# Down products of the gathered experts: three fp32r passes of split operands in place of plain fp32

## The reference

```
expert_id = g_sel[:, None] * EXPERTS_PER_GROUP + top_i
combine = sum(one_hot(expert_id, N_EXPERTS) * w2[..., None], axis=1)
out = zeros_like(h)
for n in range(N_EXPERTS):
    a, b = split(h @ w_up[n], 2, axis=-1)          # 1024 -> 2 x 256
    out = out + combine[:, n:n + 1] * ((silu(a) * b) @ w_down[n])   # 256 -> 1024
```

## Time and profile before

| | |
|---|---|
| median of 3 runs | 2070.4 us (2069.82 to 2071.71) |
| the profiled execution | 2056.48 us, span 2054.7 us |
| mean granted TensorE clock of its span | 0.962 |
| TensorE busy (matmul) | 1899.3 us, 92% of the span |
| VectorE busy | 1187.3 us, 58% |
| ScalarE busy | 787.5 us, 38% |
| DMA | 391.10 MB, mean 190 GB/s |

### The profile page before, as it was taken

The page is one execution under the profiler, slowest core; times in us unless marked ns, Lnnn a source line. Parts: engine busy times, 40 slices in busy tenths (PEclk is TensorE's granted clock), DMA queues, the critical chain, the costliest instruction groups (busy, mean ns, idle before and its releaser), DMA issues.

```text
span 2054.7 us, 30793 instructions
## 1 busy us (share of the span) xinstructions
PE 1899.3 (92%) x12768; PEld 1710.6 (83%) x12768; DVE 1187.3 (58%) x1810; ACT 787.5 (38%) x1090; POOL 201.2 (10%) x95
## 2 busy tenths in 40 slices
PE   7697889799999998999899989998999989989998
PEld 6496868678876665999888869998999987869998
DVE  1399143366665655877527548776786337546442
ACT  3334441244444444433343324333443334324332
POOL 6327700000000000000130000000000140000000
PEclk9898999799999999999999989999999999989999
DMA  8144331256699987677541046777576541032441
GB/s 268 62 144 123 124 103 41 90 195 243 246 370 382 358 312 302 248 287 286 183 144 42 22 164 228 285 289 278 197 301 267 165 137 48 22 119 110 184 185 61
DMA packets 124458, 391.10 MB, mean 190 GB/s; under 512 B 11810, under 2 KB 72532, under 8 KB 95008
## 3 DMA queue, kind: packets, MB, share of 16 engines
q1 hardware_dynamic: 122048, 387.19, 50.7%
q0 software_dynamic: 1968, 0.90, 0.2%
q10 hardware_dynamic: 304, 1.06, 0.1%
HBM read 388.06 MB, written 1.05 MB: 189 GB/s over the span
## 4 chain that ended last, share of the span: by engine, by line
PE 81%; DVE 11%; ACT 3%; issue 2%; POOL 1%; DMA 1%; DVEq 0%; SPq 0%; ACTq 0%
PE bank L544 80%; DVE region L2136 2%; PE bank L578 1%; DVE hT L1814 1%; POOL slab_low L2595 1%; DMA slab<-in_w_up 1%; DVE region L1849 1%; DVE region L2101 1%; DVE slab_low L1836 0%; DVE xT L1947 0%; ACT w_hi L1413 0%; DVE region L2112 0%; ACT L1296 0%; DVE region L2115 0%; ACT region L1318 0%
## 5 line engine op out<-in xcount | busy, mean ns | idle before, releaser
L1836 DVE TENSOR_TENSOR slab_low<-slab,w_hi 128x2048 fp32r<-128x2048 f32 x152 | 348.0, 2291 | 188.6 <-ACT w_hi L1413 188.3
L544 PE MATMUL bank<-h_hi,w_hi 128*128 128x256 f32 x1408 | 403.6, 287 | 16.3 <-DVE h_lo L1829 16.3
L544 PE MATMUL bank<-h_lo,w_hi 128*128 128x256 f32 x1408 | 401.2, 285 | 0.0
L544 PE MATMUL bank<-h_hi,slab_low 128*128 128x256 f32 x1408 | 400.3, 284 | 0.0
L1413 ACT ACTIVATE w_hi<-slab 128x2048 fp32r<-128x2048 f32 x152 | 290.4, 1912 | 156.4 <-DMA slab<-in_w_up 81.0
L544 PEld LDWEIGHTS bank<-h_hi,w_hi 128*128 128x128 f32 x1408 | 270.6, 192 | 17.8 <-issue 17.8
L544 PEld LDWEIGHTS bank<-h_hi,slab_low 128*128 128x128 f32 x1408 | 270.3, 192 | 0.0
L544 PEld LDWEIGHTS bank<-h_lo,w_hi 128*128 128x128 f32 x1408 | 269.8, 192 | 0.0
L544 PE MATMUL bank<-gT_hi,d_hi 128*128 128x256 f32 x832 | 234.2, 281 | 0.0
L544 PE MATMUL bank<-gT_hi,d_low 128*128 128x256 f32 x832 | 233.8, 281 | 0.0
L544 PE MATMUL bank<-gT_lo,d_hi 128*128 128x256 f32 x832 | 233.7, 281 | 0.0
(11 more groups left out here) (309 smaller groups left out, 3278.2 us busy)
## 6 DMA issues: line engine op xcount, KB each, us to landing
slab<-in_w_ffn_in SPq DMA_DIRECT2D x88, 1024.0 KB, 8.1
slab<-in_w_up SPq DMA_DIRECT2D x64, 1024.0 KB, 9.0
region<-in_w_ada SPq DMA_DIRECT2D x112, 512.0 KB, 6.7
region<-in_w_ffn_out SPq DMA_DIRECT2D x44, 1024.0 KB, 5.0
region<-in_w_down SPq DMA_DIRECT2D x32, 1024.0 KB, 5.5
slab<-in_w_in SPq DMA_DIRECT2D x23, 1024.0 KB, 5.4
slab<-in_w_mix_in SPq DMA_DIRECT2D x20, 1024.0 KB, 9.7
hT<-in_w_ada SPq DMA_DIRECT2D x32, 512.0 KB, 5.9
```

Of the source, the lines that this page charges most:

```text
L544: return nc.tensor.matmul(o, lhsT, rhs, start=start, stop=True, skip_group_check=True)
L1836: V_.tensor_tensor(slab_low[slot][:, :], slab[slot][:, :], w_hi[h % 3][:, :].bitcast(F), ALU.subtract)\
```

## The change

The down products of the gathered units are made like those of the full ones, in three fp32r passes. Their matmuls keep the activations as the stationary operand and 512 weight columns as the moving one. `gT_few` goes; `gT_hi`, `gT_lo`, `d_hi` and `d_low` are used for all units. ScalarE and VectorE split the down weights of every unit, and do it ahead of the first half of the next up weights; the last unit's are split in the closing slot, ahead of the turned activations. `down_few` and `bank_free` wait for the low parts.

```diff
@@ down_few
-                pe.wait_ge(S[f"d_in{b}"], 16 * (unit.u // 2 + 1))
-                pe.wait_ge(S["gt_hi"], unit.steps[-1] + 1)
+                pe.wait_ge(S["dlo_ready"], split_units(unit.u))
+                pe.wait_ge(S["gt_lo"], low_steps(unit.steps[-1]))
...
-                rows_ = d_raw[b].rearrange("p (j d) -> p j d", j=2)
+                hi = d_hi[d_hi_of(unit)][:, :].rearrange("p (j d) -> p j d", j=2)
+                lo = d_low[b][:, :].rearrange("p (j d) -> p j d", j=2)
                 for j in range(2):
                     for half in range(2):
-                        m = mm(bank[2 + half][:, :], gT_few[b][:, j, :], rows_[:, j, half * 512:(half + 1) * 512],
-                               unit.x == 0 and j == 0)
+                        o, c = bank[2 + half][:, :], slice(half * 512, (half + 1) * 512)
+                        mm(o, gT_hi[b][:, j, 0:P], hi[:, j, c], unit.x == 0 and j == 0)
+                        mm(o, gT_hi[b][:, j, 0:P], lo[:, j, c])
+                        m = mm(o, gT_lo[b][:, j, 0:P], hi[:, j, c])
@@ bank_free
-                elif unit.split:
+                else:
                     pe.wait_ge(S["gt_lo"], low_steps(old))
-                else:
-                    pe.wait_ge(S["gt_hi"], old + 1)
@@ ScalarE, slots of segment 0
+                    if unit is not None and t == 0 and unit is not members[0]:
+                        down_high(UNITS[unit.u - 1])
                     if unit is not None and t == 0:
                         up_high(unit.halves[0] + 2)
-                        if unit is not members[0] and UNITS[unit.u - 1].split:
-                            down_high(UNITS[unit.u - 1])
+                    if unit is None:
+                        down_high(members[-1])
                     for x in pending:
                         turned_high(x)
@@ VectorE, slots of segment 0
+                    if unit is not None and t == 0 and unit is not members[0]:
+                        down_low(UNITS[unit.u - 1])
                     if unit is not None and t == 0:
                         up_low(unit.halves[0] + 2)
-                        if unit is not members[0] and UNITS[unit.u - 1].split:
-                            down_low(UNITS[unit.u - 1])
+                    if unit is None:
+                        down_low(members[-1])
                     for x in pending:
                         turned_low(x)
```

More of the change, by code:

```diff
@@ L170, in split, with gathered @@
     @property
-    def split(self):
-        return self.kind != "few"
+    def gathered(self):
+        return self.kind == "few"
 def plan():
@@ L368, in build @@
         gT_lo = [parts_at(f"gT_lo{b}", [2, T], silu_at + 4096 * b + 2048) for b in range(2)]
-        gT_few = [nc.alloc_sbuf_tensor_at(f"gT_few{b}", [P, 2, P], F, offset=silu_at + 4096 * b)
-                  for b in range(2)]
         act_s, gu_s = lnt[:, 0:T], lnt[:, T:2 * T]
@@ L498, in low_steps @@
         def low_steps(s):
-            return sum(len([x for x in u.steps if x <= s]) for u in UNITS if u.split)
+            return s + 1
         def split_units(u):
-            return sum(1 for x in UNITS[:u + 1] if x.split)
+            return u + 1
         def unit_of(s):
@@ L846, in down @@
             def down(unit, middle=None):
-                if unit.split:
+                if not unit.gathered:
                     down_split(unit, unit.steps[0] == SLOTS_OF[unit.seg][0][2], middle)
@@ L1457, in turned_high @@
                     src = place(s)[:, 0:T].rearrange("p (a b) -> p a b", a=2)
-                    dst = gT_hi[b][:, :, t * P:(t + 1) * P] if unit.split else gT_few[b][:, :, :]
+                    dst = gT_hi[b][:, :, t * P:(t + 1) * P]
                     nc.scalar.activation(dst, src, ACT.Copy).then_inc(S["gt_hi"], 1)
@@ L1968, in turned_low @@
                     unit = unit_of(s)
-                    if not unit.split:
-                        return
                     b, t = unit.u % 2, s - unit.steps[0]
```

## The result

The changed kernel takes 2098.4 us (median of 4 runs, 2097.25 to 2099.61), the kernel before on the same chip 2070.1 (4 runs): ratio 1.0138, 95% interval 1.012 to 1.0155, so 28.3 us (1.4%) slower. Forecast were 2088.8 us, +18.4, with a range up to 2098.0: direction and mechanism came true, the size did not; the time lies 0.4 us above the range.

What follows compares the result with a forecast made beforehand. TensorE, with DMA just behind it, was taken to bound the kernel; its savings would all turn into waits. Dense 7.3, gathered 7.9 and tail 3.2 sum to +18.4 us, giving 2088.8 us, range 2080 to 2098.

Steps and rivals of the forecast that it cites:

- What bounds before: Gathered units: TensorE (mean 9.43 us a unit) and DMA (9.3 us) set the pace together until the adaLN pieces end.
- The down product: Each gathered unit: 12 matmuls at 0.2325 us, 2.79 us for 3.42, saving 0.63 per unit, 15.1 us in 24 units.
- Dense part: Units 0 to 7: TensorE waits for turned_low, stalls of 1.35 and 0.45 us, plus 1.4 before down(8): +7.3 us.
- Gathered part: From down(8) to down(30): a closed loop through d_hi makes 22 periods take 224.1 us against 216.2: +7.9 us.
- the period of 9.85 us: Gathered units: d_hi starts 2.99 us after the down product, the next down product 6.86 later; 18 such periods.
- The end: Last down product, down(31), waits for d_hi, d_low and gT_lo; scatter 12.95 us after down(30) instead of 9.76: +3.2 us.
- a lower granted clock comes with the new idle time: TensorE, listed among the signs that the forecast is wrong; no size given.
- rival C: Gathered part: slabs come late inside the loop, 0.5 us more in 16 periods, 2097 us; chance 0.13.
- A: TensorE still sets the pace, with new VectorE and ScalarE work under its own: faster, 2055.3 us; chance 0.06.
- B: Gathered part: DMA sets the pace and covers the loop, 2069 to 2074 us, no measurable change; chance 0.07.
- D: Only the gathered loop or only the dense stalls come true: 2081 us; chance 0.12.

Runs made afterwards that it cites:

- fastest version: The changed kernel with turned_low and the copy of y ahead of up_low, two d_hi tiles and the closing slot reordered: 2058.8 us, ratio 0.9955 to the kernel before.
- version without the waits: The changed kernel with turned_low and the copy of y ahead of up_low and a second d_hi tile for odd gathered units: 2062.1 us, ratio 0.9975.
- b_again: The kernel before, unchanged, profiled a second time: 2065.1 us, ratio 0.9981, stage 373.2 us.

## Why the prediction was right, and where it was wrong

**What bounds before.** Right as to TensorE. Half wrong as to DMA. The 0.90 at 355 GB/s was a mean over unlike stretches of before, as the first 66 us and the last 69 us of the gathered part show:

```profile
576.00:642.00 66.00, 66.00 (x255) 44.99 (x254) 43.98 (x37) 30.79 (x28) 0.00 (x0) 1.00 0.98 386
723.00:792.00 69.00, 69.00 (x264) 47.50 (x263) 37.07 (x26) 31.90 (x30) 0.00 (x0) 1.00 0.83 322
```

In the first DMA was already busy for 0.98, at 386 GB/s. In the fastest version it gives 410 over the first 73 us, 4% more than the 394 of the forecast, so a unit there takes DMA 9.0 us, and not 9.3. Whether ScalarE's waits for slabs come from this or from loads that were asked for late, no run separates.

**The down product: right.** 12 matmuls at a pitch of 0.2325 us. TensorE's busy time between down(8) and down(30) fell by 8.6 us where 22 x 0.63 = 13.9 follows from the forecast, because matmuls at half clock and the ends of bursts, which no next matmul covers, count as busy too; in the version without the waits it is 200.8 for 214.1, 13.3 less.

**Dense part: +8.6 for +7.3.** The stalls are where they were forecast, and the run with the order alone shows them alone. Each is a little larger. From one down product to the next, a unit without an adaLN sum is 1.40 to 1.47 us longer than in before where 1.35 was forecast, and one with a sum 0.66 to 0.68 where 0.45 was. The idle times shown, 1.18 and 0.42, are shorter than these shifts because they begin only at the end of the last matmul, which takes 0.39 us, while otherwise the next one starts after 0.23. With a sum the bank waits for one instruction more that I had not counted, the adaLN addition (L1938) that stands behind turned_low, but that one ends only 0.06 us later. Of the 1.3 us in all, 0.36 lie ahead of down(0), where b_again has 0.31 of them without the change.

**Gathered part: +13.4 for +7.9; the step that failed is the period of 9.85 us.** It measured 10.05. Of the 0.2, 0.15 is from the down product's start to that of d_hi (3.14 for 2.99: the first matmul of a burst takes 0.31 before the second starts, and the end of the last is seen by ScalarE 0.10 later, not 0.04) and 0.07 is from the end of gT_lo to TensorE (0.14 for 0.07). I had taken these short hops, the times from the end of an instruction to the start of the one that waits for it on another engine, from places where they were hidden in part, and multiplied them by 18. The 18 periods took 180.7 us for 177.3: 3.4 us of the 5.5. The other 2.0: the two units with a copy of y came at 10.64 and 10.66 for 10.5, and the two behind them at 14.55 and 12.97 for 12.9. The 14.55 is the first unit after a 1.88 us idle time, with the clock at 0.50 and 0.70 (windows at 670 to 674), and 1.6 us longer than its twin at full clock.

**The end: +4.5 for +3.2.** The wait before down(31) was forecast to 0.01 us (9.14 for 9.15), in part by luck: the hop to TensorE was 0.07 too short and the start of d_hi 0.07 too late. What failed is the 2.95 us of the product behind it, which ran at half clock and took 4.37.

**The clock.** The prediction named "a lower granted clock comes with the new idle time" as something that would make it wrong, but gave it no price. It came in two of the places: 1.6 + 1.4 = 3.0 us of stage.

**Sum.** Loop period 3.4, clock 3.0, dense 1.3 of the 8.1 us by which the stage's +26.5 exceeds 18.4; the last few tenths are the copies of y and rounding. So the period is the largest single term that was too small, and the clock, put at nothing, is the next; with the period right and nothing else, the forecast would have been about 2092. There is one thing more between the forecast and the 28.3 of the runs: the profile of before was not typical in its gathered part and its end. It had 216.2 and 9.8 us where b_again has 214.3 and 8.7, so a difference taken from it comes out 3 us too small. The range ended at 2098.0, put there by rival C with its late slabs. It left out that the hops had been taken at small values, and that new idle time can cost clock.

**The rivals.** A (TensorE sets the pace, 2055.3) named its own condition, turned_low ahead of a 2.21 us instruction, and the condition is what decides: with that order and the copy of y ahead too the kernel takes 2062.7, and 2058.8 with a second d_hi tile and the closing slot in order as well. The Trainium skill (Perfetto Trace Analysis, Identifying the Most-Contended Engine) says to optimize the most-contended engine first, and to judge TensorE by the share of its weight loads and not of its matmuls. By that share, too, TensorE led the compute engines in the gathered part (150.8 of 227 us, 66%, for VectorE's 61%). Here work was taken off it and the kernel became 28 us slower, and only with the queues put in order did the rule's gain show. B (DMA covers the loop) fell with even periods of 10.05 us at a DMA share of 0.87. C (late slabs) fell: ScalarE has no wait for an up slab in this stage of after. D (half of it) fell: all three parts came.

## What to carry to other kernels

Sums of busy time say whether new work fits on an engine, not what it costs: in an in-order queue a short instruction whose result the bounding engine waits for belongs ahead of long ones that only work ahead, and here 0.42 us moved past 2.28 was worth 24 us. Where a new wait closes a loop (product, split into the one tile, low part, next product), its period is the sum of every instruction and every hop between engines; read the hops from places where they are waited for, and expect them a little longer than the smallest seen. Compare the stage that was changed, cut at the same instructions, and not two spans: here 16 of 43 us between two profiles had nothing to do with the change.

## What was not expected of the hardware

- TensorE's granted clock fell to 0.50 (1.2 of 2.4 GHz) with new idle times of 1.88, 2.02, 2.2, 3.44 and 4.81 us, and cost 1.4 to 2.2 us where a down product stood behind one. But it stayed at 1.00 behind one of 1.83 us in after (755.09), and behind three of 2.09 to 2.33 us in the version with the products alone in the old order (587.18, 726.86, 768.62). So the length of the idle time alone does not tell whether the clock falls. At half clock the 512-column matmuls came 0.43 us apart instead of 0.23.
- DMA gave 410 GB/s over 73 us on this core at a share of 1.01, and 384 over 202 us at 0.96. The share of 0.90 over the whole gathered part of before had hidden that it was 0.98 in the first 66 us.
- The same code behind the stage took 1252 us in one profiled execution and 1263 or more in the other eleven. In the two of the eleven whose windows are shown above, the matmuls were busy longer, at 0.96 for 0.97 of the clock.
